# Feed-forward layers of a two-block transformer: down projections as seven block products, gate and up with tokens on partitions

## The reference

```
D_MODEL, SEQ, D_FF, DEPTH = 1024, 256, 2816, 2

def rms_norm(x, w):
    x32 = x.astype(jnp.float32)
    y = x32 * lax.rsqrt(jnp.mean(x32 * x32, axis=-1, keepdims=True) + EPS)
    return (y * w.astype(jnp.float32)).astype(x.dtype)

def swiglu(h, w_gate, w_up, w_down):
    return (jax.nn.silu(h @ w_gate) * (h @ w_up)) @ w_down

    for l in range(DEPTH):          # first_block
        x = x + 0.5 * swiglu(rms_norm(x, ffn1_norm[l]), ffn1_w_gate[l], ffn1_w_up[l], ffn1_w_down[l])
        x = x + hybrid_mixer(...)
        x = x + memory_cross_attention(...)
        x = x + 0.5 * swiglu(rms_norm(x, ffn2_norm[l]), ffn2_w_gate[l], ffn2_w_up[l], ffn2_w_down[l])
```

## Time and profile before

| | before |
|---|---|
| median of 3 runs | 2333.3 us (2333.22 to 2333.4) |
| profiled execution, first to last instruction | 2332.8 us |
| PE busy | 2318.1 us, 99% of the span |
| DVE busy | 1550.0 us, 66% |
| ACT busy | 1194.5 us, 51% |
| DMA queue of the weights | 412.73 MB, 55.3% of the 16 engines' time |
| granted TensorE clock, mean | 0.999 of full |
| matmuls | 13587 |

### The profile page before, as it was taken

The page is one execution under the profiler, slowest core; times in us unless marked ns, Lnnn a source line. Parts: engine busy times, 40 slices in busy tenths (PEclk is TensorE's granted clock), DMA queues, the critical chain, the costliest instruction groups (busy, mean ns, idle before and its releaser), DMA issues.

```text
span 2332.8 us, 34527 instructions
## 1 busy us (share of the span) xinstructions
PE 2318.1 (99%) x13587; PEld 2000.9 (86%) x13587; DVE 1550.0 (66%) x1454; ACT 1194.5 (51%) x1207; POOL 17.6 (1%) x15
## 2 busy tenths in 40 slices
PE   9999999999999999999999999999999999999999
PEld 8888889888888898888888888888888888888887
DVE  6667866666666677666667666476667667467666
ACT  5446456544544565655445445655445445565444
POOL 0000010000000001000000000000000000000000
PEclk9999999999999999999999999999999999999999
DMA  8656544555556564536556565546565556555653
GB/s 297 195 188 179 158 145 154 179 191 191 187 190 197 174 186 148 177 129 216 191 180 228 187 195 191 162 149 209 192 192 188 188 193 194 180 163 170 200 188 118
DMA packets 330987, 428.02 MB, mean 183 GB/s; under 512 B 17608, under 2 KB 296400, under 8 KB 330640
## 3 DMA queue, kind: packets, MB, share of 16 engines
q1 hardware_dynamic: 324832, 412.73, 55.3%
q10 hardware_dynamic: 6064, 13.98, 1.7%
HBM read 425.61 MB, written 1.05 MB: 183 GB/s over the span
## 4 chain that ended last, share of the span: by engine, by line
PE 97%; DVE 2%; ACT 1%; DMA 0%; issue 0%; ACTq 0%; DVEq 0%
PE ps L1144 25%; PE ps L1030 18%; PE ps L1031 18%; PE ps L1032 18%; PE ps L1148 13%; PE ps L1043 1%; PE ps L1343 0%; DVE wlo L1710 0%; PE ps L1412 0%; PE ps L1422 0%; DMA xres<-in_x 0%; PE ps L1569 0%; PE ps L1383 0%; PE ps L1263 0%; ACT arena L888 0%
## 5 line engine op out<-in xcount | busy, mean ns | idle before, releaser
L1710 DVE TENSOR_TENSOR wlo<-raw,whi 128x2048 fp32r<-128x2048 f32 x390 | 892.9, 2291 | 495.9 <-ACT whi L518 495.4
L518 ACT ACTIVATE whi<-raw 128x2048 fp32r<-128x2048 f32 x392 | 746.6, 1906 | 592.7 <-PE ps L1032 364.7
L1144 PE MATMUL ps<-hT,whi 128*128 128x512 f32 x2560 | 610.8, 390 | 0.0
L1144 PEld LDWEIGHTS ps<-hT,whi 128*128 128x128 f32 x2560 | 474.9, 188 | 95.1
L1030 PE MATMUL ps<-whi,hT 128*128 128x512 f32 x920 | 368.7, 401 | 1.3 <-DVE hT L2232 1.1
L1032 PE MATMUL ps<-whi,hT 128*128 128x512 f32 x920 | 359.4, 391 | 0.0
L1031 PE MATMUL ps<-wlo,hT 128*128 128x512 f32 x920 | 358.7, 390 | 0.0
L1148 PEld LDWEIGHTS ps<-hT,wlo 128*128 128x128 f32 x2560 | 329.3, 191 | 13.1
L1148 PE MATMUL ps<-hT,wlo 128*128 128x256 f32 x2560 | 333.3, 283 | 0.0
L1030 PE MATMUL ps<-whi,aT_hi 128*128 128x512 f32 x640 | 250.0, 391 | 0.0
L1031 PE MATMUL ps<-wlo,aT_hi 128*128 128x512 f32 x640 | 249.9, 391 | 0.0
(11 more groups left out here) (299 smaller groups left out, 1906.0 us busy)
## 6 DMA issues: line engine op xcount, KB each, us to landing
raw<-in_w_ffn SPq DMA_DIRECT2D x264, 512.0 KB, 4.3
raw<-in_w_in SPq DMA_DIRECT2D x144, 512.0 KB, 4.8
raw<-in_ffn_w_down SPq DMA_DIRECT2D x88, 512.0 KB, 4.2
raw<-in_ffn_w_up SPq DMA_DIRECT2D x86, 512.0 KB, 4.0
raw<-in_ffn_w_gate SPq DMA_DIRECT2D x86, 512.0 KB, 4.9
raw<-in_w_out SPq DMA_DIRECT2D x32, 512.0 KB, 4.1
gain<-in_gains ACTq DMA_DIRECT2D x16, 512.0 KB
raw<-in_cross_wk SPq DMA_DIRECT2D x16, 512.0 KB, 4.4
```

Of the source, the lines that this page charges most:

```text
L518: act.activation(whi[:, s, :, 0:cols], raw[:, s, :, 0:cols], ACT.Copy).then_inc(hi_ready, 1)
L1144: pe.matmul(ps[:, G + n, :], whi[:, s, k, n * P:(n + 1) * P], both[k], start=first and k == 0, stop=False, skip_group_check=True)
L1710: dve.tensor_tensor(wlo[:, s, :, 0:cols], raw[:, s, :, 0:cols], whi[:, s, :, 0:cols].bitcast(F32), ALU.subtract).then_inc(lo_ready, 1)
```

## The change

Two things change in each of the eight feed-forward parts.

**Gate and up.** In steps 1 to 10 the wide form is gone. `half_tokens` takes one block of 128 tokens: `hT_hi` and `hT_lo` are stationary, 512 columns of `whi` are streamed against each, then 512 columns of `wlo` against `hT_hi`: 12 matmuls of 512 columns for each half of the inputs and each token block. Both token blocks of a step go one after the other through the one bank 4 (`G`); in step 1 the first goes through bank 7. ACT must take the first token block out of the bank (`first_evac`, a silu and a scaled copy, counter `up_out`) before PE writes the second. The token factor is again a scale per partition, so the row and its two transposes go (`ROWS` from 3 to 1), and DVE's `sums` go. In return the product has to be transposed in every step (`turn_act`, four PE transposes, into bank 4 as well).

**Down.** In steps 0 to 8 the 2 x 2 x 2 blocks (tokens, features, outputs) of the down product are made from seven block products in place of eight, from sums and differences of activation blocks (`parts_sums`, DVE) and of weight blocks (`block_sums`, DVE). A product is three matmuls, so a step has 21 in place of 24. The seven products accumulate over nine steps in banks 0 to 3 and 5 to 7, each in its own, and are then added to or taken from pieces of `xres` by 11 `flush` additions on DVE. The 21 matmuls of a step are put in three places (`CHUNKS`): nine before the transposes of the next step, seven behind them, and five between the two token blocks of the step after. Steps 9 and 10 keep the normal form with 24 matmuls. The factor and the 0.5 now go into the product (`hinv`), so the last addition has the factor 1.0.

```
+BLOCKED = FF_STEPS - 2
+BLOCKS = ((0, 0, 0, 0), (1, 0, 2, 1), (6, 0, 1, 2), (4, 1, 0, 3), (3, 1, 1, 5), (5, 2, 0, 6), (2, 2, 1, 7))
+CHUNKS = (0, 9, 16, 21)
...
-ROWS = (3, 3)
+ROWS = (1, 1)
...
# SP
+            def load_blocks(b, l, off, c, parts, n):
+                s = slot_of(b, l, off)
+                sp.wait_ge(block_summed, 3 * n + 3)
...
# ACT
+                def block_hi(g, j, c=0):
+                    n, o = BLOCKED * f + j + c, off + 4 + 3 * j
+                    s = slot_of(b, l, o)
+                    if g == 0:
+                        act.wait_ge(raw_loaded[s], 32 * (use(b, l, o, c) - (s < 2)))
...
+                        src = raw[:, s, 1:4, :]
+                    else:
+                        act.wait_ge(block_summed, 3 * n + (1, 3)[g - 1])
...
+                        src = block_sum[:, 2 * g - 2:2 * g, :]
+                    act.activation(blocks_of(b, l, o, g)[0], src, ACT.Copy).then_inc(block_hi_ready, 1)
+                def first_evac(stp, c=0, bank=G):
+                    act.wait_ge(first_half, WIDE * f + stp + c)
+                    act.activation(silu_g[:, 0, :], ps[:, bank, 0:256], ACT.Silu, scale=stat[:, 0, 2, 0:1]).then_inc(silu_done, 1)
+                    act.activation(prod[:, 0, :], ps[:, bank, 256:512], ACT.Copy, scale=hinv[:, 0:1]).then_inc(up_out, 1)
+                def step_(stp, c=0, last=False):
+                    first_evac(stp, c)
+                    block_hi(1, stp - 1, c)
+                    parts_hi(stp - 1, c)
+                    block_hi(2, stp - 1, c)
+                    split_hi(b, l, off + 2 + 3 * stp, c)
+                    second_silu(stp, c)
+                    split_hi(b, l, off + 3 + 3 * stp, c, units=1 if last else 2)
+                    take_parts(stp, c)
+                    if not last:
+                        block_hi(0, stp, c)
...
# PE
-                for n0, n1 in ((0, 2), (2, 4)) if gate_first else ((0, 4),):
-                    tiles = [(n, k) for n in range(n0, n1) for k in range(4)]
-                    for n, k in tiles:
-                        pe.matmul(ps[:, G + n, :], whi[:, s, k, n * P:(n + 1) * P], both[k], start=first and k == 0, stop=False, skip_group_check=True)
...
+                for k in range(4):
+                    pe.matmul(ps[:, bank, :], hT_hi[:, t, k0 + k, :], whi[:, s, k, :], start=first and k == 0, stop=False, skip_group_check=True)
+                    pe.matmul(ps[:, bank, :], hT_lo[:, t, k0 + k, :], whi[:, s, k, :], start=False, stop=False, skip_group_check=True)
+                if t == 0:
+                    wait_weights(b, l, off, c)
+                for k in range(4):
+                    mm = pe.matmul(ps[:, bank, :], hT_hi[:, t, k0 + k, :], wlo[:, s, k, :], start=False, stop=last and k == 3, skip_group_check=True)
...
+                def step_(stp, c=0, first=False, last=False):
+                    pe.wait_ge(parts_out, WIDE * f + stp + c)
+                    gate_up(stp, 0, c)
+                    blocks(stp - 2, 2, c, first)
+                    pe.wait_ge(up_out, WIDE * f + stp + c)
+                    gate_up(stp, 1, c)
+                    blocks(stp - 1, 0, c, False, last)
+                    turn_act(stp, c)
+                    blocks(stp - 1, 1, c, False, last)
...
+                gate_up(1, 0, bank=TR + 1)
+                turn_act(0, bank=ACC + 1)
+                gate_up(1, 1)
+                pe.wait_ge(up_out, WIDE * f + 1)
+                blocks(0, 0, first=True)
+                turn_act(1)
+                blocks(0, 1, first=True)
...
# DVE
+                def block_sums(j, c=0):
...
+                    dve.tensor_tensor(block_sum[:, 0:2, :], r[:, 1:3, :], r[:, 0, :].unsqueeze(1).broadcast_to([P, 2, 512]), ALU.add).then_inc(block_summed, 1)
...
+                def step_(stp, c=0, last=False):
+                    parts_sums(stp - 1, c)
+                    block_lo(0, stp - 1, c)
+                    block_sums(stp - 1, c)
+                    kept_product(stp, c)
+                    block_lo(1, stp - 1, c)
+                    parts_lo(stp - 1, c)
+                    block_lo(2, stp - 1, c)
+                    bank_product(stp, c)
+                    split_lo(b, l, off + 2 + 3 * stp, c)
+                    split_lo(b, l, off + 3 + 3 * stp, c, units=1 if last else 2)
...
+                def flush(n, bank, i, sign, after):
+                    if after:
+                        dve.wait_ge(flushed, FLUSHES * f + after)
+                    src = ps[:, bank, :] if bank is not None else first_two[:, 1, :]
+                    dve.tensor_tensor(piece(xres, i), piece(xres, i), src, ALU.add if sign else ALU.subtract).then_inc(flushed, 1)
```

More of the change, by code:

```diff
@@ L682, in ffn @@
+                act.wait_ge(act_turned, FF_STEPS * (f + 1))
+                act.activation(aT_hi[:, :, :, :], ps[:, G, :].rearrange("p (k t c) -> p k t c", k=2, t=TB), ACT.Copy).then_inc(act_hi, 1)
                 if more:
@@ L1264, in turn_act @@
                     mm.then_inc(act_turned, 1)
-                def down(off, c, step, first, last):
-                    lhs = from_hT(4) if last else lambda k: (aT_hi[:, k], aT_lo[:, k])
-                    pe.wait_ge(act_lo, FF_STEPS * f + step + 1)
-                    tall_unit(b, l, off, lhs, ACC, first, last, c, signal=acc_done if last else None,
-                              then=turn_ahead(b, T_next) if last else {},
-                              order=LAST_ORDER if last and T_next is None else range(PIECES))
@@ L1273, in step_, with gate_up @@
-                def step_(off, c, step, gate_first=False):
-                    pe.wait_ge(up_sum, WIDE * f + step - 1)
-                    for k in range(2):
-                        wide_unit(b, l, off + k, c, 4 * k, k == 0, k == 1, gate_first and k == 1)
-                    down(off + 2, c, step - 1, False, False)
+                def gate_up(stp, t, c=0, bank=G):
+                    u = off - 1 + 3 * stp
+                    mm = half_tokens(b, l, u, c, 0, t, bank, True, False)
+                    if t:
+                        mm.then_inc(unit_done, 1)
+                    half_tokens(b, l, u + 1, c, 4, t, bank, False, True).then_inc(unit_done if t else first_half, 1)
@@ new lines, in blocks @@
+                def blocks(j, chunk, c=0, first=False, last=False):
+                    o = off + 4 + 3 * j
+                    if chunk == 0:
+                        pe.wait_ge(act_lo, FF_STEPS * f + j + c + 1)
+                    for i in range(CHUNKS[chunk], CHUNKS[chunk + 1]):
+                        m, part = divmod(i, 3)
+                        at, g, q, bank = BLOCKS[m]
+                        hi, lo = blocks_of(b, l, o, g)
+                        if part == 0 and m in (0, 3, 5):
+                            pe.wait_ge(block_lo_ready, 3 * (BLOCKED * f + j + c) + g + 1)
+                        mm = pe.matmul(ps[:, bank, :], (part_lo if part == 1 else part_hi)[:, at * P:(at + 1) * P], (lo if part == 2 else hi)[:, q, :],
+                                       start=first and part == 0, stop=last and part == 2, skip_group_check=True)
+                        if i in (8, 14):
+                            mm.then_inc(block_used, 1)
+                    if chunk == 2:
+                        mm.then_inc(unit_done, 1)
```

316 lines of the change are left out of this document (205 added, 111 removed).

## The result

The changed kernel takes 2343.26 us (median of 4 runs, 2342.58 to 2344.01), the kernel before 2333.35 us beside it (4 runs, 2333.22 to 2333.66): a ratio of 1.0043, 95% interval 1.0028 to 1.0057. It is slower by 9.9 us. I had forecast 2326, with a range of 2313 to 2343 and most of the chance on faster. The time lies just outside the range, 0.3 us above its end, and the sign is wrong.

What follows compares the result with a forecast made beforehand. PE was taken to bound the kernel (busy 99%). Terms -15 - 49 + 34 - 2 + 21 + 4 = -7 us took the span from 2332.8 to 2326; forecast 2326 us, range 2313 to 2343 (8 in 10).

Steps and rivals of the forecast that it cites:

- PE's own work: PE's matmuls and transposes over 8 parts: gate/up -15, down -49, transposes +34, token-factor row -2; sum -32 us without waits.
- the handover: Steps 2 to 10: PE waits for ACT to empty bank 4 before the second token block, 0.06 x 72 = +4 us.
- The starts: Start of each part: PE waits for DVE's split of the activation parts, 2.0 to 4.3 us each, 20.7 us in sum.
- The clock: Rival: after the 2 to 4 us waits at part starts the clock falls, +9 us, 2336; chance 0.05.
- My main case: All terms as laid out, giving 2326 us, with its own range of 2317 to 2335; chance 0.70.
- The rest of a round is covered: Loop round of 16.19 us: DVE's 14.3 and ACT's 10.4 us fit, no other PE wait, narrowest margin 0.5 us.
- The two rivals on the fast side and at 2348: Starts covered, PE alone counts: about 2302, chance 0.07; DVE sets the round, +22 us: about 2348, chance 0.08.
- The gap by the page: Warm matmul gap of N/2.4 + 2.5 ns, which would make PE's sum an estimated -18 us; measured distances were used instead.
- a dearer handover: Rival: emptying bank 4 between token blocks takes ACT longer; at 0.3 us a step +17, about 2343; chance 0.10.

Runs made afterwards that it cites:

- experiment 9: Changed kernel, loop rounds: the 21 block-product matmuls take their stationary operand from `hT_hi` and `hT_lo` instead of the activation parts; 2340.18 us, one run.
- Experiments 1 and 2: Changed kernel: 1 splits activation parts before block sums and later blocks, 2333.3 us; 2 also moves ACT's copy of transposed product between its weight splits, 2319.49 us.
- experiment 3: Changed kernel with dummy matmuls of 512 columns filling PE's waits at the start of each part; 2338.61 us, ratio 1.0022 to the kernel before.
- experiment 4: Changed kernel with seven instead of five block-product matmuls between the two token blocks of a step; 2343.78 us, ratio 1.0042 to the kernel before.

## Why the prediction was wrong, step by step

- **PE's own work, -32 us: mis-sized, the step that failed.** I took 0.2275 us for every matmul of 512 columns, from a down unit of 5.46 us, and wrote myself that a changed distance would prove me wrong. That unit is 0.23 at its head and 0.2267 behind it, and I did not look inside it. Block products are 0.2325 apart all along, and the token blocks beside them take 5.48 to 5.50 instead of 5.46: a round of 16.30 to 16.33, not 16.19. Eight rounds of this are 1.0 us a part. The comparison of the parts gives 1.5 us a part, 12 us in all; the other 0.5 lies in the steps at both ends of a part and was not broken down. So this term and the handover, -28 us together, came out as -16. Why block products are slower stays open but for the nine (experiment 9). The terms themselves (27 matmuls fewer, transposes at 0.43) were right. They gave 4.0 us a part before any wait, and 1.5 of it went here.
- **The starts, +20.7 us: right in place, cause and size.** 19.5 us, by part 3.03, 1.80, 1.80, 3.32, 4.17, 1.79, 1.79 and 1.79, against 2.9, 2.0, 2.0, 3.5, 4.3 and three times 2.0. Experiments 1 and 2 confirm that it is a matter of order. Laying out DVE's row instruction by instruction from durations of the trace gave waits to 0.2 us.
- **The clock: the rival to which I gave 0.05.** I saw a fall after waiting near the program's start, priced it at +9 and then held it for unlikely, since no long wait within the work was in the trace. Its condition came true and its price was near: of 6.3 us by the comparison of the parts, 4.6 stand behind the two longest waits, and experiment 3 gives about 5 us back. The other 1.7 are the fall at 308, which is not shown to come from the waits at the starts. My main case put this at nothing, though the same waits that it contained were the condition of this rival, so it should not have been a case beside the others but a likely addition to the main one.
- **The handover, +4 us: at most 1.5 us of it seen.** PE does start a matmul 0.04 us late at that place, 72 times (bars of 0.43), and ACT's copy is the last to release it. But with the wait out of the way the round is shorter by 0.02 us on the mean, and in the part shown not at all (experiment 4).
- **The rest of a round is covered: right.** No wait of PE in a round but this; DVE is busy for 1815 us, I had said about 1850. DVE sets no round.
- **The two rivals on the fast side and at 2348** did not happen: the starts were not covered, and DVE's row fits.

- **The gap by the page.** I took 0.216 and 0.109 us from the section "Back-to-back issue gap" of the Trainium skill's page "TensorE: Matmul & The Clock Gate". The section calls this the gap of an isolated matmul, and gives about 131 ns at 512 columns for a stream of them. The even stretches of this case are at 226.7 ns, so that figure is further off than the one that I used.

The sum: my -32 + 4, plus 12 that the rounds took beyond these two, plus 19.5 (starts) and 6.3 (clock), less 1 for the first load, is +8.8, against +9.0 in the spans. The mis-sized term alone turned the sign: without the lower clock the kernel would still have been about 3 us slower than before. That 2343.26 missed my range by only 0.3 us is luck: the range was that wide for a dearer handover and for DVE's row, and neither was the reason. My 0.5 us between the span and the time was too small: the profiled execution took 2343.6 us, 1.8 above its span, and the 43 executions of the kernel before that ran beside the experiments show 1.8 to 2.1. Both kernels have it, so it does not touch the difference of the two.

## What to carry to other kernels

When a change puts a new operation between the bound engine's work, write out the other engines' rows up to the step *behind* the first wanted result, and order each row by when its results are wanted: here two changes of order were worth 22 us, where the whole change had been meant to give 7. A wait of the matmul engine of a few microseconds costs more than itself, since the clock may fall and stay down after it; price it together with the wait. And where a gain is three matmuls in 24, a distance taken from the old operands is not good enough: 0.11 to 0.14 us on a round of 69 such matmuls, with what the ends of a part added, gave back more than a third of PE's gain.

## What the runs showed of the hardware

- The granted clock went to 0.50 within or right after an idle stretch of PE of 3.3 and 4.2 us, and stayed there up to 5.6 us into the work. Waits of 1.8 us left it alone in the profiled run of the changed kernel; in that of experiment 4, whose starts are the same, stretches with 0.83 and 0.87 follow the waits that end at 36 and 646 us, the latter one of the waits of 1.8 us. So which waits are followed by a fall differs from run to run. A fall behind short waits of 1.2 and 0.8 us, near 306 us, stands in some traces and not in others. The Trainium skill, page "TensorE: Matmul & The Clock Gate", section "Part 1: The HAM clock gate", has the clock depend on activity; the traces agree, and experiment 3 shows it from the other side, dummy work giving 5 us back.
- Matmuls of the same 512 columns are not always the same distance apart. Nine fill 2.10 us with the stationary operand from the tile `rounded` and 2.04 us with it from `hT`, with the same widths, types and banks. Twelve others, whose moving operand also lies in `rounded`, kept 1.72 us (seven) and 1.17 us (five) when their stationary operand was changed in the same way.
- A row of such matmuls starts slower than it goes on: 0.23 us apart for the first six of a down unit of before, 0.2267 for the other eighteen. The order of the three matmuls of a product, one bank for all, or a change of bank at every matmul made no difference (2.10, 2.10, 2.11 us for nine).
- Four transposes between matmuls of 512 columns cost about 0.43 us, measured by leaving them out (rounds of 15.89 beside 16.32 to 16.34 us in one run).
